# Attention whose value matmul turns around: values with ones columns as weights, one normalisation per head, no turns of the result

## The chip, the cores and the metric

The kernel runs on 1 core of one Trainium2 chip. The metric is the time of one execution on the device in microseconds (us), as a median over runs.

## What is computed

The program is a stack of transformer blocks for 512 tokens of width 1024. The change lies in the first mixer, an attention with 16 heads whose query and key have 96 numbers per head (64 without and 32 with rotary positions) and whose value has 64:

```python
q = (rms_norm(q_lat, q_norm) @ w_qb).reshape(B, S, H, QK_NOPE + QK_ROPE)
kv = (rms_norm(kv_lat, kv_norm) @ w_kvb).reshape(B, S, H, QK_NOPE + V_HEAD)
...
s = (jnp.einsum('bqhd,bkhd->bhqk', qn, k_nope)
     + jnp.einsum('bqhr,bkr->bhqk', qr, k_rope)).astype(jnp.float32) * scale
s = jnp.where(causal, s, MASK_VALUE)
p = jax.nn.softmax(s, axis=-1).astype(v.dtype)
...
o = jnp.einsum('bhqk,bkhd->bqhd', p, v)   # for each block of 128 queries
return o @ w_out
```

Everything is float32. The projections are done as three matmuls on two halves of each number (`hi` and `lo`), so each weight is split before its use: ScalarE makes `whi`, VectorE `wlo`.

## The kernel before, in words

The order on each engine is the order in which `mla_pe`, `mla_act` and `mla_dve` write it; semaphores alone tie the engines together. The heart is a loop of 68 steps over 64 units. A unit is one head `h` and one block `i` of 128 queries (`mla_units`); by causality it has `i + 1` blocks of keys, so its width is 128, 256, 384 or 512 columns. Eight steps, two heads, make a group; "position" below is the step number modulo 8, so positions 3 and 7 hold the widest units. In step `n`

- TensorE does the scores of unit `n`, turns the probabilities of unit `n-3` (`turn`, a transpose per key block), and multiplies those of unit `n-4` with the values (`values`). Between these come the matmuls of the next group's query and key projection (`mla_project`): ten triples of 512 columns, up to three of them in a step from position 1 on.
- VectorE adds the mask and takes the row maximum (one custom instruction, `prob<-ps,tab`), scales it (L347, the event `nm`), takes reciprocals of the row sums, and in between works at `modulation` (`part<-stage`, two instructions of 256 columns in a step, from step 2 to step 49), the lower halves of the weights (`dve_ahead`), and `queries` (four instructions of rotary work for two heads).
- ScalarE does the exponential with the row sum (`prob<-prob`), copies the turned probabilities to `probt`, the result times the reciprocal to `mlao` (`L.O`), splits weights and copies `mlaqh` and `mlakh`.

PSUM banks are handed out in turn by `take` and `banks`: five banks rotate over scores, turned probabilities and results, so whoever takes a bank waits until its use five takes ago is free. After the loop, 32 transposes turn `L.O`, ScalarE and VectorE split the outcome in `xhi` and `xlo`, then split the first pieces of `w_out`, and the output projection `wo` begins.

## Time and profile before

| | us |
|---|---|
| median of 3 runs | 3034.06 (3028.78 to 3034.18) |
| the profiled execution, its own time | 3029.49 |
| its span, first to last instruction | 3028.2 |
| TensorE busy | 2824.6 |
| VectorE busy | 1716.8 |
| ScalarE busy | 1235.5 |

Busy times are those of the whole program; the attention loop is the stretch from 110.2 to 297.0 us of the span. The profiled execution lies at the lower end of the runs.

### The profile page before, as it was taken

What the parts mean: (1) busy time and instruction counts of PE and PEld (TensorE: products, weight loads), DVE (VectorE), ACT (ScalarE), POOL (GpSimd) and SP (SyncE); (2) the same over time, 40 slices, a digit from 0 to 9 for tenths busy, and PEclk for the clock granted to TensorE, in tenths of its full rate; (3) what the DMA queues carried; (4) which work ended last, traced back from release to release, by engine and by line L of the source; (5) the groups of instructions that cost most, each with busy time, mean ns of one, the idle gap of its engine ahead of it and who ended that gap; (6) DMA issues with size and microseconds to landing.
All of it is one profiled execution on the core that took longest, in us unless ns stands there. A gap on an engine that the chain in (4) does not pass through costs nothing. (4 is left out here: it accounts for less than half of the span.)

```text
span 3028.2 us, 36283 instructions
## 1 busy us (share of the span) xinstructions
PE 2824.6 (93%) x14489; PEld 2311.1 (76%) x14489; DVE 1716.8 (57%) x2889; ACT 1235.5 (41%) x2128; POOL 247.4 (8%) x224
## 2 busy tenths in 40 slices
PE   7988999999997989899999997999999998899998
PEld 5766787787886978678877775788788766678886
DVE  6675554445864866543578886443425386744344
ACT  3556322223434344333467775432233345432222
POOL 0000000000003442010000010121100002100000
PEclk9899999999999999899999998999999999999999
DMA  5232344332231211154589994211330214422321
GB/s 227 89 110 87 111 182 153 132 113 89 106 138 42 71 43 43 50 204 146 188 317 360 345 369 156 81 49 60 101 113 32 84 35 134 144 72 87 112 80 66
DMA packets 72096, 387.66 MB, mean 128 GB/s; under 512 B 8234, under 2 KB 9934, under 8 KB 36174
## 3 DMA queue, kind: packets, MB, share of 16 engines
q1 hardware_dynamic: 58512, 349.20, 31.7%
q10 hardware_dynamic: 10382, 26.07, 2.5%
q0 software_dynamic: 3024, 9.98, 0.9%
q8 instruction: 116, 1.90, 0.3%
q14 instruction: 62, 0.51, 0.1%
HBM read 368.43 MB, written 22.03 MB: 129 GB/s over the span
## 5 line engine op out<-in xcount | busy, mean ns | idle before, releaser
L343 DVE TENSOR_TENSOR wlo<-stage,whi 128x1024 fp32r<-128x1024 f32 (+3 forms) x504 | 531.4, 1095 | 354.7 <-ACT whi L355 347.7
L355 ACT ACTIVATE whi<-stage 128x1024 fp32r<-128x1024 f32 (+3 forms) x504 | 440.5, 922 | 225.4 <-PE ps L639 195.5
L639 PE MATMUL ps<-bxhi,whi 128*128 128x512 f32 x480 | 200.9, 419 | 17.1 <-DVE bxlo L343 8.4
L639 PE MATMUL ps<-whi,mxhi 128*128 128x512 f32 (+1 forms) x528 | 204.3, 387 | 9.4 <-DVE wlo L343 7.3
L639 PE MATMUL ps<-whi,mxlo 128*128 128x512 f32 (+1 forms) x528 | 197.5, 374 | 0.0
L639 PE MATMUL ps<-wlo,mxhi 128*128 128x512 f32 (+1 forms) x528 | 197.4, 374 | 0.0
L639 PE MATMUL ps<-bxhi,wlo 128*128 128x512 f32 x480 | 190.1, 396 | 0.0
L639 PE MATMUL ps<-bxlo,whi 128*128 128x512 f32 x480 | 189.7, 395 | 0.0
L343 DVE TENSOR_TENSOR wlo<-more,whi 128x1024 fp32r<-128x1024 f32 (+1 forms) x126 | 142.2, 1171 | 44.3 <-ACT whi L355 43.7
L351 DVE SCALAR_TENSOR_TENSOR part<-stage,small,part 128x256 f32<-128x256 f32 x259 | 151.1, 583 | 9.2
L639 PE MATMUL ps<-lxhi,whi 128*128 128x512 f32 x352 | 141.2, 401 | 6.1 <-DVE lxlo L351 5.0
L639 PE MATMUL ps<-gwide 128*128 128x128 f32 x1088 | 134.3, 283 | 13.2 <-POOL gwide L343 10.2
L639 PE MATMUL ps<-fxhi,whi 128*128 128x512 f32 x352 | 139.7, 397 | 5.0 <-DVE fxlo L351 3.8
L639 PEld LDWEIGHTS ps<-gwide 128*128 128x128 f32 x1088 | 128.8, 197 | 16.2 <-POOL gwide L343 12.8
L639 PE MATMUL ps<-fxhi,wlo 128*128 128x512 f32 x352 | 138.6, 394 | 0.0
L639 PE MATMUL ps<-fxlo,whi 128*128 128x512 f32 x352 | 138.3, 393 | 0.0
L639 PE MATMUL ps<-lxhi,wlo 128*128 128x512 f32 x352 | 137.8, 391 | 0.0
L639 PE MATMUL ps<-lxlo,whi 128*128 128x512 f32 x352 | 137.7, 391 | 0.0
L355 ACT ACTIVATE whi<-more 128x1024 fp32r<-128x1024 f32 (+1 forms) x126 | 121.1, 1011 | 39.0 <-PE ps L639 36.0
L639 PEld LDWEIGHTS ps<-whi,mxhi 128*128 128x128 f32 x528 | 99.9, 189 | 38.5 <-DVE wlo L343 16.0
L639 PEld LDWEIGHTS ps<-bxhi,whi 128*128 128x128 f32 x480 | 91.9, 192 | 37.9 <-DVE bxlo L343 9.2
L639 PEld LDWEIGHTS ps<-whi,mxlo 128*128 128x128 f32 x528 | 99.9, 189 | 18.2
(597 smaller groups left out, 6283.9 us busy)
## 6 DMA issues: line engine op xcount, KB each, us to landing
stage<-in_gu SPq DMA_DIRECT2D x92, 1024.0 KB, 5.7
stage<-in_ada SPq DMA_DIRECT2D x40, 1024.0 KB, 5.0
more<-in_gu SPq DMA_DIRECT2D x40, 1024.0 KB, 6.7
stage<-in_dn SPq DMA_DIRECT2D x26, 768.0 KB, 4.5
stage<-in_dn SPq DMA_DIRECT2D x19, 1024.0 KB, 6.6
stage<-in_gin SPq DMA_DIRECT2D x16, 1024.0 KB, 4.9
stage<-in_gt SPq DMA_DIRECT2D x16, 1024.0 KB, 4.9
more<-in_dn SPq DMA_DIRECT2D x13, 1024.0 KB, 7.0
```

The source lines that it names most:

```text
L343: return e.do.tensor_tensor(out, x, y, op)
L351: return e.do.scalar_tensor_tensor(out, x, c, y, op0, op1)
L355: return e.do.activation(out, x, f, **kw)
L639: return self.p.do.matmul(out, lhsT, rhs, start=start, stop=stop, skip_group_check=True)
```

## The change

The value matmul swaps its operands. The values of a pair of heads now lie in SBUF as 64 columns of one head, 64 columns of ones, 64 columns of the other (`L.V`, the ones written once by GpSimd in `mla_pool`). A slice of 128 of these columns is the stationary operand, and the turned probabilities (128 columns) move. The result comes out turned, one PSUM bank per head for all four query blocks (`("oh", h)`, banks 3 and 4 by turns), with the row sums in the other 64 partitions. So the exponential no longer sums, the reciprocals and the copies to `mlao` go, and so do the 32 transposes after the loop. Once per head, behind its fourth block, ScalarE takes Ln and Exp(-x) of the row sums (`share`) and VectorE multiplies the head with them into `L.OT` (`weigh`). Scores and turned probabilities now rotate over three banks. On ScalarE the copy of unit `n-3` stands ahead of the exponential of unit `n`. The projections are spread over positions 1 to 6; the split of the key weights and the query work move to position 4, the key copies to position 6. The split of the result (`across_act`, `dve_low`) and the first two pieces of `w_out` move into steps 56 to 63.

```diff
@@ -834,8 +834,12 @@
         L = Space()
         L.X = tuple(self.at(n, [P, 8, 512], o, F32R) for n, o in (("xhi", 46), ("xlo", 54)))
         L.XK = tuple(t[:, 4:6, :] for t in L.X)
-        L.V, L.O = self.at("mlav", [P, 4, 1024], 62), self.at("mlao", [P, 4, 1024], 70)
-        L.raw = L.O[:, :, :].rearrange("p a b -> p (a b)").rearrange("p (m n) -> p m n", n=512)
+        L.V = self.at("mlav", [P, 4, 8, 192], 62)
+        ot = self.at("mlao", [P, 4, 512], 74)
+        early = [self.at(n, [P, 2, 512], o) for n, o in (("mlaoa", 52), ("mlaob", 60))]
+        L.OT = [early[i % 2][:, i // 2, :] for i in range(4)] + [ot[:, i, :] for i in range(4)]
+        low = self.at("mlaraw", [P, 4, 512], 84)
+        L.raw = [low[:, i, :] for i in range(4)] + [ot[:, i, :] for i in range(4)]
         L.cs = self.at("rope", [P, 2, 512], 78)
         L.q = [self.at("mlaq", [96, 4, 512], 80)[:, i, :] for i in range(1)]
         q, k = self.at("mlaqh", [96, 4, 512], 80), self.at("mlakh", [96, 4, 512], 84)
...
@@ -894,7 +899,7 @@
         self.pe_gemm_tok("wv", "wv", range(4), L.XE, self.normed("nk"))
         for _ in self.mla_project(L, 0):
             pass
-        self.banks(range(5))
+        self.banks(range(3))
         units = self.mla_units()
         more = None
 
@@ -915,35 +920,31 @@
 
         def values(n):
             h, i = units[n]
-            ps, vacant = self.take(("o", n))
-            p.wait_ge(*vacant, A(free(("t", n))), A(("v", h // 4, 3)))
+            if i == 0:
+                _, vacant = self.take(("oh", h), at=3 + h % 2)
+                p.wait_ge(*vacant)
+            ps, side = self.bank(("oh", h)), slice(64 * (h % 2), 64 * (h % 2) + 128)
+            p.wait_ge(A(free(("t", n))), A(("v", h // 4, 3)), self.G("ones"))
             for j in range(i + 1):
-                z = self.mm(ps[:, 0:64], L.pt[n % 4][:, j * P:(j + 1) * P], L.V[:, j, h * 64:h * 64 + 64], j == 0, j == i)
+                z = self.mm(ps[:, i * P:(i + 1) * P], L.V[:, j, h // 2, side], L.pt[n % 4][:, j * P:(j + 1) * P], j == 0, j == i)
             z.then_inc(*P_.up(("o", n)))
 
         for n in range(64 + 4):
-            if n % 8 == 0 and n < 56:
-                more = self.mla_project(L, n // 8 + 1)
-            step = more if n % 8 and n < 64 else iter(())
+            if n % 8 == 0:
+                more = self.mla_project(L, n // 8 + 1) if n < 56 else iter(())
             if n < 64:
                 scores(n)
-            next(step, None)
+            if n % 8 in (1, 2, 3, 4):
+                next(more, None)
             if 3 <= n < 67:
                 turn(n - 3)
-            next(step, None)
+            if n % 8 in (1, 2, 3, 4, 5, 6):
+                next(more, None)
             if n > 3:
                 values(n - 4)
-            next(step, None)
             if n >= 8 and (n - 8) % 4 == 0 and (n - 8) // 4 < 12:
                 self.pe_ada(0, 8 + (n - 8) // 4)
         self.banks(range(7))
-        for m in range(8):
-            ps, vacant = self.take(("ot", m))
-            p.wait_ge(*vacant)
-            for i in range(4):
-                p.wait_ge(A(free(("o", 4 * (2 * m + 1) + i))))
-                z = self.tr(ps[:, i * P:(i + 1) * P], L.O[:, i, m * P:(m + 1) * P])
-            z.then_inc(*P_.up(("ot", m)))
         for _ in self.pe_gemm("wo", "wo", range(4), L.X, lambda q: [V(("ot", "l", q))]):
             pass
...
@@ -1016,23 +1018,22 @@
                 k = (2 * g + h) % 4
                 act(a, L.k[k][0:64, :], self.bank(use)[64 * h:64 * h + 64, :], ACT.Copy).then_inc(*A.up(("ke", 2 * g + h), *([free(use)] if h else [])))
 
+        def share(h):
+            top, low = slice(64 * (h % 2), 64 * (h % 2) + 64), slice(64 - 64 * (h % 2), 128 - 64 * (h % 2))
+            r = L.tmp[2][top, :]
+            a.wait_ge(P_(("o", 4 * h + 3)), *([V(("od", h - 2))] if h > 1 else [V(("nq", "l", 3))]))
+            act(a, r, self.bank(("oh", h))[low, :], ACT.Ln).then_inc(*A.up())
+            a.wait_ge(A.now())
+            act(a, r, r, ACT.Exp, scale=-1.0).then_inc(*A.up(("share", h)))
+
         units = self.mla_units()
         self.act_ahead("wq", 0)
         queries(0)
         self.act_ahead("wk0", 0)
         keys(0)
+        self.act_ahead("wq", 1, False)
         for n in range(64 + 4):
             g = n // 8 + 1
-            if n < 64:
-                w = (units[n][1] + 1) * P
-                c, sl = L.cols[n % 6], L.sl[n % 5]
-                a.wait_ge(V(("nm", n)))
-                act(a, sl[:, 0:w], sl[:, 0:w], ACT.Exp, bias=c[:, 5:6], scale=L.scale, accum_out=c[:, 4:5]).then_inc(*A.up(("e", n)))
-            if n % 8 == 2 and g < 8:
-                self.act_ahead("wq", g, False)
-                self.act_ahead(f"wk{g}", 0, False)
-            if n % 8 == 4 and g < 8:
-                keys(g)
             if 3 <= n < 67:
                 u = n - 3
                 w = (units[u][1] + 1) * P
@@ -1040,26 +1041,43 @@
                 if u >= 4:
                     a.wait_ge(P_(("o", u - 4)))
                 act(a, L.pt[u % 4][:, 0:w], self.bank(("t", u))[:, 0:w], ACT.Copy).then_inc(*A.up(free(("t", u))))
-            if n % 8 == 3 and g < 8:
+            if n < 64:
+                w = (units[n][1] + 1) * P
+                sl = L.sl[n % 5]
+                a.wait_ge(V(("nm", n)))
+                act(a, sl[:, 0:w], sl[:, 0:w], ACT.Exp, bias=L.cols[n % 6][:, 5:6], scale=L.scale).then_inc(*A.up(("e", n)))
+            if n % 8 == 4 and g < 8:
+                self.act_ahead(f"wk{g}", 0, False)
                 queries(g)
+            if n % 8 == 6 and g < 8:
+                keys(g)
...
             if n > 3:
-                u = n - 4
-                h, i = units[u]
-                a.wait_ge(P_(("o", u)), V(("rl", u)))
-                if u < 4:
-                    a.wait_ge(V(("nk", "l", 1)))
-                act(a, L.O[:, i, h * 64:h * 64 + 64], self.bank(("o", u))[:, 0:64], ACT.Copy, scale=L.cols[u % 6][:, 6:7]).then_inc(*A.up(free(("o", u))))
+                h, i = units[n - 4]
+                if i == 3:
+                    share(h)
             if n % 8 == 7 and g < 7:
                 self.act_ahead("wq", g + 1, False)
-        for m in range(8):
-            if m == 0:
-                a.wait_ge(P_(("o", 63)))
-            self.act_high("ot", L.X, m, self.bank(("ot", m))[:, :], P_(("ot", m)))
+            if 56 <= n < 63:
+                self.across_act(L, n - 56)
+            if n in (61, 63):
+                self.act_ahead("wo", 0, n == 63)
+        self.across_act(L, 7)
         for n in range(4):
             self.act_ahead("wo", n)
             for m in (2 * n, 2 * n + 1):
                 self.act_square("wo", m, L.tmp[0:2], 1.0, *([V("posread")] if m == 0 else []))
         self.last_square = L.tmp[1], A(("wo", "q", 7))
+
+    def across_act(self, L, m):
+        marks = [self.V(("od", 2 * m)), self.V(("od", 2 * m + 1)), self.P((("k", 7), 0))]
+        if m > 5:
+            marks.append(self.V(("ot", "l", m - 6)))
+        self.act_high("ot", L.X, m, L.OT[m], *marks)
+
+    def mla_pool(self, L):
+        g = self.g
+        g.wait_ge(self.V(("mod", 0, 1)))
+        g.do.memset(L.V[:, :, :, 64:128], 1.0).then_inc(*self.G.up("ones"))
 
     def rope_angles(self, L, between):
         v, V, A = self.v, self.V, self.A
...
@@ -1157,6 +1175,7 @@
         self.dve_ahead("wq", 0)
         queries(0)
         self.dve_ahead("wk0", 0)
+        self.dve_ahead("wq", 1, False)
         v.wait_ge(self.Dt[0]("tab"))
 
         def modulation():
@@ -1164,6 +1183,12 @@
                 yield from self.dve_ada(0, n)
                 if n % 4 == 0 and n > 8:
                     self.dve_mod(0, n // 4 - 1)
+
+        def weigh(h):
+            top = slice(64 * (h % 2), 64 * (h % 2) + 64)
+            b = self.bank(("oh", h))
+            v.wait_ge(A(("share", h)))
+            tt(v, L.OT[h // 2][top, :], b[top, :], L.tmp[2][top, :], MUL).then_inc(*V.up(("od", h), free(("oh", h))))
 
         more = modulation()
         for n in range(64 + 4):
@@ -1174,31 +1199,30 @@
                 v.wait_ge(P_(("s", n)))
                 if n >= 5:
                     v.wait_ge(P_(("t", n - 5)))
-                if n >= 6:
-                    v.wait_ge(A(free(("o", n - 6))))
                 v.do.tensor_tensor_reduce(sl[:, 0:w], self.bank(("s", n))[:, 0:w], L.tab[:, 512 - w:512], 1.0, NEG, ADD, MAX, c[:, 0:1]).then_inc(
                     *V.up(free(("s", n))))
                 v.wait_ge(V.now())
                 ts(v, c[:, 5:6], c[:, 0:1], -L.scale, None, MUL).then_inc(*V.up(("nm", n)))
-            if n % 8 == 2 and g < 8:
-                self.dve_ahead("wq", g, False)
+            if n % 8 == 4 and g < 8:
                 self.dve_ahead(f"wk{g}", 0, False)
-            if n % 8 == 3 and g < 8:
                 queries(g)
             if n > 3:
-                c = L.cols[(n - 4) % 6]
-                v.wait_ge(A(("e", n - 4)))
-                v.do.reciprocal(c[:, 6:7], c[:, 4:5]).then_inc(*V.up(("rl", n - 4)))
+                h, i = units[n - 4]
+                if i == 3:
+                    weigh(h)
             if n % 8 == 7 and g < 7:
                 self.dve_ahead("wq", g + 1, False)
             if n > 1:
                 next(more, None)
+            if 56 <= n < 63:
+                self.dve_low("ot", L.X, n - 56, L.OT[n - 56])
+            if n in (61, 63):
+                self.dve_ahead("wo", 0, n == 63)
         for _ in more:
             pass
         self.dve_mod(0, 4)
         self.dve_gain("n2", 0, 3, "nf0")
-        for m in range(8):
-            self.dve_low("ot", L.X, m, self.bank(("ot", m))[:, :], P_(("ot", m)), done=[free(("ot", m))])
+        self.dve_low("ot", L.X, 7, L.OT[7])
         for n in range(4):
             self.dve_ahead("wo", n)
```

The first place is VectorE from the mask of position 3 on (`ISA prob` is the mask and maximum, `part<-stage` the modulation, `tmp<-ps,rope` and `mlaqh<-tmp` the query work). Before:

```order
L1179 ISA prob,small<-ps,tab 128x512 [waits s_matmuls]
L1179 ISA small 128x1
L347 TENSOR_SCALAR small<-small 128x1 [waits s_vector]
L343 TENSOR_TENSOR tmp<-ps,rope 64x512 [waits s_vector,s_matmuls]
L343 TENSOR_TENSOR tmp<-ps,rope 64x512
L343 TENSOR_TENSOR mlaqh<-tmp 32x512 [waits s_vector]
L343 TENSOR_TENSOR mlaqh<-tmp 32x512
L1191 RECIPROCAL small<-small 128x1
L351 SCALAR_TENSOR_TENSOR part<-stage,small,part 128x256 [waits s_vector] x2
```

In the changed kernel:

```order
L1202 ISA prob,small<-ps,tab 128x512 [waits s_matmuls]
L1202 ISA small 128x1
L347 TENSOR_SCALAR small<-small 128x1 [waits s_vector]
L343 TENSOR_TENSOR mlaob<-ps,tmp 64x512 [waits s_scalar]
L351 SCALAR_TENSOR_TENSOR part<-stage,small,part 128x256 [waits s_vector] x2
L1202 ISA prob,small<-ps,tab 128x128 [waits s_matmuls]
L1202 ISA small 128x1
L347 TENSOR_SCALAR small<-small 128x1 [waits s_vector]
L343 TENSOR_TENSOR wlo<-stage,whi 128x128 [waits s_scalar] x2
L343 TENSOR_TENSOR tmp<-ps,rope 64x512 [waits s_vector,s_matmuls]
L343 TENSOR_TENSOR tmp<-ps,rope 64x512
```

The multiplication with the share (`mlaob<-ps,tmp`), which waits for ScalarE, and the split of the key weights now stand ahead of the query work, and the mask of the next unit too.

The second place is ScalarE there, from the exponential of the widest unit on. Before:

```order
L355 ACTIVATE prob,small<-prob,small 128x512 [waits s_vector]
L355 ACTIVATE probt<-ps 128x128 [waits s_matmuls]
L355 ACTIVATE mlaqh<-ps 64x512 x2
L355 ACTIVATE mlao<-ps,small 128x64 [waits s_vector,s_matmuls]
L355 ACTIVATE prob,small<-prob,small 128x128 [waits s_vector]
L355 ACTIVATE mlakh<-ps 64x512 [waits s_matmuls]
L355 ACTIVATE mlakh<-ps 64x512
L355 ACTIVATE probt<-ps 128x256 [waits s_matmuls]
```

In the changed kernel:

```order
L355 ACTIVATE prob<-prob,small 128x512 [waits s_vector]
L355 ACTIVATE tmp<-ps 64x512 [waits s_matmuls]
L355 ACTIVATE tmp<-tmp 64x512 [waits s_scalar]
L355 ACTIVATE probt<-ps 128x256 [waits s_matmuls]
L355 ACTIVATE prob<-prob,small 128x128 [waits s_vector]
L355 ACTIVATE whi<-stage 128x128 [waits s_load2]
L355 ACTIVATE whi<-stage 128x128
L355 ACTIVATE mlaqh<-ps 64x512 x2
```

The Ln and the Exp of `share` (`tmp<-ps`, `tmp<-tmp`) follow the widest exponential; the key weights and the queries follow the next one.

The third place is TensorE at positions 4 and 5 (`small,prob` are the transposes, `mlav,probt` the values, `xhi,whi` a projection). Before:

```order
L642 MATMUL ps<-small,prob 128x128 x2
L639 MATMUL ps<-mlav,probt 128x64 [waits s_vector]
L639 MATMUL ps<-small,part 128x1 x2
L639 MATMUL ps<-mlakh,mlaqh 128x256
L642 MATMUL ps<-small,prob 128x128 [waits s_scalar]
L642 MATMUL ps<-small,prob 128x128 x2
L639 MATMUL ps<-mlav,probt 128x64 [waits s_scalar,s_vector]
L639 MATMUL ps<-mlav,probt 128x64
```

In the changed kernel:

```order
L642 MATMUL ps<-small,prob 128x128 [waits s_vector]
L642 MATMUL ps<-small,prob 128x128
L639 MATMUL ps<-xhi,whi 128x512
L639 MATMUL ps<-xlo,whi 128x512
L639 MATMUL ps<-xhi,wlo 128x512
L639 MATMUL ps<-probt,mlav 128x128 [waits s_scalar]
L639 MATMUL ps<-small,part 128x1 x2
L639 MATMUL ps<-mlakh,mlaqh 128x256
L642 MATMUL ps<-small,prob 128x128 [waits s_vector]
L642 MATMUL ps<-small,prob 128x128 x2
```

The transposes waited for ScalarE (`s_scalar`) and now wait for VectorE (`s_vector`), because of the rotation over three banks: `turn` takes the bank of the scores of the step before, which VectorE's mask frees.

## Rows read from the trace of the kernel before

**Rows 1.** The page: busy us, share of the span and instructions by engine.

```profile
PE 2824.6 (93%) x14489; PEld 2311.1 (76%) x14489; DVE 1716.8 (57%) x2889; ACT 1235.5 (41%) x2128; POOL 247.4 (8%) x224
```

**Rows 2.** Window: length, busy PE, PEld, DVE, ACT, POOL, clock, DMA, GB/s.

```profile
149.40:221.60 72.20, 60.83 (x344) 46.72 (x343) 52.36 (x170) 40.13 (x120) 0.00 (x0) 1.00 0.32 115
```

**Rows 3.** Two windows of 4 us early in the loop, same columns.

```profile
116.00:120.00 4.00, 2.29 (x10) 1.23 (x8) 3.25 (x9) 2.16 (x5) 0.00 (x0) 1.00 0.01 2
...
124.00:128.00 4.00, 3.32 (x12) 2.32 (x11) 1.83 (x8) 2.22 (x7) 0.00 (x0) 0.50 0.37 124
```

**Rows 4.** Timeline of PE: the score matmul that opens step 24, 32, 48, 56.

```profile
181.76 0.44 PE L639 MATMUL ps<-mlakh,mlaqh 96*128 96x128 f32 x2
...
205.81 0.44 PE L639 MATMUL ps<-mlakh,mlaqh 96*128 96x128 f32 x2
...
256.52 0.44 PE L639 MATMUL ps<-mlakh,mlaqh 96*128 96x128 f32 x2
...
279.52 0.44 PE L639 MATMUL ps<-mlakh,mlaqh 96*128 96x128 f32 x2
```

**Rows 5.** Timeline of PE, steps 21 to 28: values, the widest score, waits, one triple.

```profile
177.36 0.63 PE L639 MATMUL ps<-mlav,probt 128*128 128x64 f32 x4 [1.70 <-ACT probt L355]
...
179.58 1.08 PE L639 MATMUL ps<-mlakh,mlaqh 96*128 96x512 f32 x2
...
187.02 0.63 PE L639 MATMUL ps<-mlav,probt 128*128 128x64 f32 x4 [0.94 <-ACT probt L355]
...
194.43 1.00 PE L639 MATMUL ps<-mlav,probt 128*128 128x64 f32 x8
...
196.18 0.50 PE L639 MATMUL ps<-xhi,whi 128*128 128x512 f32 x1 [0.75 <-ACT mlaqh L355]
...
196.98 0.39 PE L639 MATMUL ps<-mlakh,mlaqh 96*128 96x128 f32 x2
```

**Rows 6.** Timeline of DVE, steps 23 to 28.

```profile
180.70 0.69 DVE L1179 CUSTOM_DVE_ANT_0 prob<-ps,tab 128x512 f32<-128x512 f32 x1 [0.30 <-ACT probt L355]
...
183.35 1.29 DVE L343 TENSOR_TENSOR wlo<-stage,whi 128x512 fp32r<-128x512 f32 x2 [1.70 <-ACT whi L355]
...
191.26 0.49 DVE L343 TENSOR_TENSOR wlo<-stage,whi 128x128 fp32r<-128x128 f32 x2 [1.42 <-ACT whi L355]
...
194.63 1.41 DVE L343 TENSOR_TENSOR tmp<-ps,rope 64x512 f32<-64x512 f32 x2 [0.61 <-PE ps L639]
...
196.07 1.40 DVE L343 TENSOR_TENSOR mlaqh<-tmp 32x512 f32<-32x512 f32 x2
...
197.70 1.01 DVE L351 SCALAR_TENSOR_TENSOR part<-stage,small,part 128x256 f32<-128x256 f32 x2
...
198.74 0.29 DVE L1179 CUSTOM_DVE_ANT_0 prob<-ps,tab 128x128 f32<-128x128 f32 x1
```

**Rows 7.** Timeline of ACT, the same steps.

```profile
181.62 0.72 ACT L355 ACTIVATE prob<-prob,small 128x512 f32<-128x512 f32 x1 [0.71 <-DVE small L347]
...
199.26 0.40 ACT L355 ACTIVATE prob<-prob,small 128x128 f32<-128x128 f32 x1 [1.19 <-DVE small L347]
```

**Rows 8.** Tile prob before the loop: a Ln out of PSUM, then an Exp (min/median/max ns).

```profile
L355 ACT ACTIVATE prob<-ps,small x2: 687/688/689, 34.5 to 66.4; 128x512 f32<-128x512 f32 x2
...
L355 ACT ACTIVATE prob<-prob x2: 630/630/631, 35.2 to 67.1; 128x512 f32<-128x512 f32 x2
```

**Rows 9.** Timeline of PE in a later stage: 128-column fp32 matmuls, eight back to back.

```profile
1073.38 1.06 PE L639 MATMUL ps<-qkv 128*128 128x128 f32 x8
```

**Rows 10.** Timeline of PE, ACT and DVE from the last values to the projection.

```profile
296.82 3.85 PE L642 MATMUL ps<-small,mlao 128*128 128x128 f32 x32
...
304.27 0.47 PE L639 MATMUL ps<-xhi,whi 128*128 128x512 f32 x1 [3.60 <-DVE wlo L343]
...
301.44 3.95 ACT L355 ACTIVATE whi<-stage 128x1024 fp32r<-128x1024 f32 x4
...
302.91 4.62 DVE L343 TENSOR_TENSOR wlo<-stage,whi 128x1024 fp32r<-128x1024 f32 x4
```

More of the change, by code:

```diff
@@ L856, in mla @@
                     (), [self.P(("sqx", 7))])
-        L.nq = Norm("nq", lambda m: L.raw[:, m, :], 4, L.rq, self.prm["qn"], None, L.X, L.tmp,
+        L.nq = Norm("nq", lambda m: L.raw[m], 4, L.rq, self.prm["qn"], None, L.X, L.tmp,
                     lambda m: [L.raw_ok(m)], [self.A("rsq")], (), [self.P(("win", 6))], [self.V("krope"), self.P("sumq")])
-        L.nk = Norm("nk", lambda m: L.raw[:, 4 + m, :], 2, L.rs, self.prm["kvn"], None, L.XE, [L.raw[:, 6, :], L.raw[:, 7, :]],
+        L.nk = Norm("nk", lambda m: L.raw[4 + m], 2, L.rs, self.prm["kvn"], None, L.XE, [L.raw[6], L.raw[7]],
                     lambda m: [L.raw_ok(4 + m)], [self.A("rsk")])
```

12 lines of the change are left out of this document (7 added, 5 removed).

## Prediction

> **What bounds the kernel now.** I read the page first: TensorE is busy for 93% of the span [rows 1], so most of the program is bound by TensorE, and what the change does counts only where TensorE waits. The reader should see that the attention loop is such a place: over 72.2 us (three groups) TensorE is busy for 60.8, VectorE for 52.4 and ScalarE for 40.1, at a granted clock of 1.00 [rows 2]. None is full, so three engines wait for each other in a ring. The timeline gives the length of a group: step 24 opens at 181.76 and step 32 at 205.81, so 24.05 us; the group without modulation work (steps 48 to 55) takes 279.52 - 256.52 = 23.0 [rows 4]. TensorE's waits in a group are 1.70, 0.94 and 0.75 [rows 5], and one of 0.32 beside them that isn't shown: 3.7 in all. The two largest, before values, end with ScalarE's copy to `probt`, which stood behind an exponential that waited for VectorE (1.19 at 199.26) [rows 7]. VectorE in turn waited 1.70 and 1.42 for `whi` [rows 6]. After the loop TensorE spends 3.85 on 32 transposes, idles 3.60 more, and starts the output projection at 304.27 [rows 10], 24.75 after step 56 opened [rows 4].
>
> **The value matmul costs the same.** Before, 160 fp32 matmuls of 64 moving columns, eight instructions (four matmuls) in 1.00; now 128 columns move. The nearest row for that shape is a later stage: eight instructions of 128 columns take 1.06 [rows 5, 9]. So 0.015 for each matmul, 160 x 0.015 = 2.4 at most over the whole loop, and 0 if only the tail of the last one differs. I take 0; the other bound is that of a rate in proportion to the columns, which the same two rows exclude. The Trainium skill, TensorE: Matmul & The Clock Gate, section on the back-to-back issue gap, gives an isolated gap that grows with the moving columns, N / 2.4 GHz + 2.5 ns: four passes of 64 more columns would by it be an estimated 0.107 us for each of 160 matmuls, 17 us in all. The same page puts a weight load of 128 columns at 128 / 1.2 = 107 ns, and by that the load, not the moving side, paces both forms; rows 5 and 9 agree with that.
>
> **What goes.** Eight reciprocals in a group (I price one at 0.1: under 1 us of VectorE), the read of the row sum and the copy to `mlao` on ScalarE. None lies where the new ring closes, so 0 on the path. The ScalarE copy ahead of the exponential removes the waits of 1.70 and 0.94 as they stand. The 32 transposes (3.85) and the 3.60 idle after them go from the end.
>
> **What comes.** Once per head Ln and Exp on ScalarE, 0.69 + 0.63 [rows 8], with hops of some 0.05 to each side 1.4; then the multiplication on VectorE out of PSUM, nearest row `tmp<-ps,rope`, 1.41 / 2 = 0.7 [rows 6]. VectorE's own work in a group thus grows by only 1.4 - 0.8, to about 18. But `weigh` of a head stands in the very step in which TensorE ends that head's last values, so VectorE stops for it, and behind it are queued the modulation, the next mask and, at position 4, the key weights and queries. Who waits for the masks is TensorE: with three banks `turn` of unit n-3 takes the bank of the scores of step n-1, so the transposes need the mask of the step before. Before, the five banks put that demand only on the values, a little later in the step. GpSimd writes the ones before the loop, when VectorE has nothing on the path: 0; if that cover were gone, one write of 2048 columns, a few us at most by POOL's other work.
>
> **One group of the changed kernel**, from the end of the values at position 7:
> - A. ScalarE is 0.4 late (the score at position 7 ends 1.2 before the values; mask to exponential 181.62 - 180.70 = 0.9 and exponential 0.7 follow it [rows 6, 7]); share 1.4; multiply 0.7; lower halves of the query weights 1.3; modulation 1.0; mask 0.3: TensorE's transposes at position 1 may start after 5.1.
> - B. TensorE from there to the end of the values at position 3. Before, 187.02 to 195.43 is 8.4 with six triples [rows 5]; now five (a triple 196.98 - 196.18 = 0.8 with its start, 0.7 in a row) and three transposes of 0.12 each (3.85 / 32 [rows 10]): 8.4 - 0.7 + 0.4 = 8.1.
> - C. Share 1.4; multiply 0.7; modulation 1.0; mask start to exponential 199.26 - 198.74 = 0.5; exponential 0.3; `whi` of the key weights 0.5 and VectorE's last half of them 0.3; queries 1.41 + 1.40 = 2.8; modulation 1.0; mask of 256 columns 0.5 [rows 6 to 8]. Sum 9.0, all in series, since each waits for the one before or stands behind it.
> - D. TensorE again: four transposes 0.5, the tenth triple 0.7, three value matmuls 0.7, the widest score 1.0 (1.08 with its tail [rows 5]), two transposes 0.2, four value matmuls 1.0: 4.1.
>
> Sum 26.3, against 24.05: +2.3. Steps 8 to 47 are five such groups, +11.5. In steps 48 to 55 the modulation ends after two steps, which takes 1.0 off A or C twice: 24.3 against 23.0, +1.3. The first group has one share only, at its end: 0. The loop up to step 56: +12.8.
>
> **The last steps.** From step 56 on no projection covers anything, and each step carries a split: exponential, `xhi` on ScalarE (0.5, as the Exp of 512 columns, 0.63, less its overlap with the next [rows 8]), then `xlo` on VectorE (0.65, as half of 1.29 [rows 6]), then the next mask, for which the transposes wait. Mask start to the next mask start is 0.5 + 0.3 + 0.5 + 0.7 = 2.0 for 128 columns, 2.3 and 2.6 for the next two, and 0.9 + 0.6 + 1.4 (share) + 1.3 = 4.2 for 512. The first mask waits for the share and multiplication of head 12: 2.5. Then 2.0 + 2.3 + 2.6 + 4.2 + 2.0 + 2.3 + 2.6 = 18.0, plus the first piece of `w_out` in step 61 (`whi` 3.95 / 4 = 1.0 and `wlo` 2.35 for two [rows 10], less the 0.7 it replaces: 2.6). Step 63: exponential 1.5 after its mask, share 1.4, two `whi` 2.0; then the copies and values of the last three units, 2.8. Together 30.8 from step 56 to the first matmul of the projection, against 24.75: +6.1. So the removed 7.3 at the end is paid with longer steps before it. The share of head 15 lies behind nine microseconds of matmuls that don't need it: 0.
>
> **Sum.** 12.8 + 6.1 = +18.9 on the profiled execution's 3029.49: 3048.4. That execution is 4.6 below the median of the runs; on the median it is 3053, which I forecast.
>
> **Rivals.**
> - *TensorE closes the loop (faster).* If VectorE reaches the masks in time, the transposes never wait and a group is TensorE's own work, 24.05 - 3.7 = 20.35, so -3.7 x 7 = -26; the last steps keep their 17.5 and lose 7.3: about 3001 by the median. For it: VectorE's work of 18 is under 20.35. It decides in C: the stretch from share to mask of position 5 must be under the TensorE work beside it, about 5 us (score, two triples, transposes, values); the rows give 9.0. Half of it (only position 3 stalls) lands near 3020. Chance 0.17.
> - *The ends cancel.* If VectorE makes up at positions 1 and 2 what it loses, a group stays near 24 and the last steps come out within 4 of before: 3028 to 3040. Chance 0.12.
> - *TensorE's clock falls more often.* The changed loop lets TensorE idle about 6 in 26 instead of 3.7 in 24, in gaps of 1.5 to 2. Before, TensorE was busy for only 2.29 of the 4.0 us from 116 on, and at 124 the clock stood at 0.50, that is at 1.2 GHz [rows 3]. B and D then run at half speed: about 12 us of a group. One fall of some 10 us in each of four more groups costs 4 x 4 = 16 more: 3062 to 3080. Chance 0.15. The Trainium skill (TensorE: Matmul & The Clock Gate, "What's actually happening") says that idleness brings the lower level and activity lifts it; the rows fit, since the fall came behind a pause.
> - *The forecast*, a ring over share, multiplication and masks: 3040 to 3064. Chance 0.53, and 0.03 for something slower still.
>
> A measurement of this kernel can tell about 0.2%, 6 us. Faster is the first rival with its half case, 0.17; same 0.12; slower 0.71. The range of 8 in 10 leaves out the faster rival's lower part and the clock's upper part: 3016 to 3074; the likeliest case alone is 3040 to 3064. The unknown costs (0 to 2.4 of the value matmul, 0.1 to 0.2 for each hop, some 12 in the ring: +-1 a group) lie inside.
>
> **What would show it.** After: step 24 to step 32 some 26 us; TensorE's longest waits before transposes (L642) ended by VectorE's mask; VectorE's longest wait ended by ScalarE's Exp in `tmp`, about 3 us at position 3; value matmuls 1.0 for eight; the first `xhi,whi` of the projection right behind the last values, 30 us after step 56 opens. Wrong if groups are 22 or less, if the transposes wait for nothing, or if eight value instructions take nearer 1.8.

## The result, and the profile after

The changed kernel takes 3062.7 us (median of 4 runs, 3059.74 to 3064.55) against 3034.12 for the kernel before (3028.78 to 3040.47). The ratio is 1.0096, 95% interval 1.0072 to 1.0121: some 29 us slower. The forecast was 3053, its likeliest case 3040 to 3064. The profiled execution of the changed kernel took 3063.30, its span 3062.0.

The page first, the rows that answer to [rows 1]; the columns are busy time, share of the span, instructions.

```profile
## 1 busy us (share of the span) xinstructions
PE 2839.1 (93%) x14457; PEld 2320.2 (76%) x14457; DVE 1722.4 (56%) x2841; ACT 1237.5 (40%) x2032; POOL 248.4 (8%) x225
```

They tell almost nothing: VectorE's and ScalarE's work is that of before within 6 us. The stretch of [rows 2] says more, and behind it stands one group, step 24 to step 32, cut into slices of 4 us. The columns are the length, each engine's busy time with its instructions, TensorE's granted clock, the DMA share and GB/s.

```profile
149.40:221.60 72.20, 56.61 (x289) 43.21 (x289) 48.62 (x134) 35.70 (x72) 0.00 (x0) 0.90 0.27 99
...
184.77:212.64 27.87, 21.55 (x117) 16.60 (x115) 18.07 (x51) 13.76 (x29) 0.00 (x0) 0.94 0.27 100
...
188.00:192.00 4.00, 2.86 (x9) 2.18 (x10) 3.75 (x13) 1.39 (x4) 0.00 (x0) 0.73 0.03 8
192.00:196.00 4.00, 4.00 (x21) 3.31 (x20) 2.28 (x7) 1.26 (x3) 0.00 (x0) 0.84 0.43 141
...
216.00:220.00 4.00, 2.99 (x10) 2.22 (x11) 3.75 (x13) 1.38 (x4) 0.00 (x0) 0.65 0.02 4
220.00:224.00 4.00, 4.00 (x13) 3.00 (x12) 2.15 (x7) 0.22 (x1) 0.00 (x0) 0.50 0.50 156
```

Every engine does less in the same 72.2 us than in [rows 2]: the loop waits more. And the clock, 1.00 in [rows 2], is now 0.90 over this stretch of some three groups, down to 0.50 in one slice. The next fence is TensorE's timeline through that group, the rows that answer to [rows 4, 5]; in brackets stand the idle time before an instruction and what ended it.

```profile
184.77 0.39 PE L639 MATMUL ps<-mlakh,mlaqh 96*128 96x128 f32 x2
...
188.26 0.50 PE L639 MATMUL ps<-xhi,whi 128*128 128x512 f32 x1 [1.78 <-DVE wlo L343]
...
190.11 0.90 PE L642 MATMUL ps<-small,prob 128*128 128x128 f32 x3 [0.89 <-DVE small L1202]
...
198.62 1.05 PE L639 MATMUL ps<-probt,mlav 128*128 128x128 f32 x8
199.51 0.39 PE L639 MATMUL ps<-mlakh,mlaqh 96*128 96x128 f32 x2
...
203.11 0.55 PE L642 MATMUL ps<-small,prob 128*128 128x128 f32 x3 [0.48 <-DVE small L1202]
205.23 0.50 PE L639 MATMUL ps<-xhi,whi 128*128 128x512 f32 x1 [1.57 <-DVE tmp L343]
...
208.91 0.66 PE L642 MATMUL ps<-small,prob 128*128 128x128 f32 x4 [1.61 <-DVE small L1202]
...
211.75 1.05 PE L639 MATMUL ps<-probt,mlav 128*128 128x128 f32 x8
212.64 0.39 PE L639 MATMUL ps<-mlakh,mlaqh 96*128 96x128 f32 x2
```

The group is 27.87 long (24.05 before). The waits before values are gone, as foreseen, and three waits now stand before the transposes (L642), each ended by VectorE's mask and maximum (L1202), with two more before triples, ended by VectorE too. Eight value instructions start 0.89 ahead of what follows them (211.75 to 212.64), though twice as many columns move; in the kernel before it was 0.91:

```profile
180.85 1.08 PE L639 MATMUL ps<-mlav,probt 128*128 128x64 f32 x8
181.76 0.44 PE L639 MATMUL ps<-mlakh,mlaqh 96*128 96x128 f32 x2
```

What VectorE did meanwhile in the changed kernel, from its timeline:

```profile
200.99 0.69 DVE L343 TENSOR_TENSOR mlaoa<-ps,tmp 64x512 f32<-64x512 f32 x1 [2.79 <-ACT tmp L355]
201.72 1.00 DVE L351 SCALAR_TENSOR_TENSOR part<-stage,small,part 128x256 f32<-128x256 f32 x2
202.76 0.29 DVE L1202 CUSTOM_DVE_ANT_0 prob<-ps,tab 128x128 f32<-128x128 f32 x1
...
203.91 0.49 DVE L343 TENSOR_TENSOR wlo<-stage,whi 128x128 fp32r<-128x128 f32 x2 [0.67 <-ACT whi L355]
204.51 1.41 DVE L343 TENSOR_TENSOR tmp<-ps,rope 64x512 f32<-64x512 f32 x2
205.95 1.40 DVE L343 TENSOR_TENSOR mlaqh<-tmp 32x512 f32<-32x512 f32 x2
207.38 1.00 DVE L351 SCALAR_TENSOR_TENSOR part<-stage,small,part 128x256 f32<-128x256 f32 x2
208.42 0.42 DVE L1202 CUSTOM_DVE_ANT_0 prob<-ps,tab 128x256 f32<-128x256 f32 x1
```

It stands still for 2.79, for ScalarE's Ln and Exp of the row sums, and from 200.99 it works up to the mask at 208.42 that TensorE wants, with one more pause, of 0.67, for ScalarE's `whi` of the key weights. That is the ring of the prediction's part C.

The end of the loop, TensorE and ScalarE:

```profile
295.76 0.39 PE L639 MATMUL ps<-mlakh,mlaqh 96*128 96x128 f32 x2
...
324.69 1.22 PE L639 MATMUL ps<-probt,mlav 128*128 128x128 f32 x4 [3.97 <-ACT probt L355]
325.70 1.06 PE L642 MATMUL ps<-small,prob 128*128 128x128 f32 x4
326.55 3.19 PE L639 MATMUL ps<-probt,mlav 128*128 128x128 f32 x14
329.40 0.67 PE L639 MATMUL ps<-xhi,whi 128*128 128x512 f32 x1
```

```profile
321.08 0.59 ACT L355 ACTIVATE tmp<-ps 64x512 f32<-64x512 f32 x1
321.70 0.63 ACT L355 ACTIVATE tmp<-tmp 64x512 f32<-64x512 f32 x1
322.24 1.98 ACT L355 ACTIVATE whi<-stage 128x1024 fp32r<-128x1024 f32 x2
324.25 0.77 ACT L355 ACTIVATE probt<-ps 128x256 f32<-128x256 f32 x2
```

The projection starts 33.64 after step 56 opens (24.75 before). Set against the profiled execution of before, the 25.1 by which it starts later come together like this: the first group (110.2 to 127.73) is 17.53 in place of 22.74, -5.2; steps 8 to 47 take 142.14 (127.73 to 269.87) in place of 123.60, +18.5; steps 48 to 55 take 25.89 in place of 23.0, +2.9; and the end +8.9.

### The profile page after: what moved, and what is told of

Same layout as the page of the kernel before. It is cut to its first block and busy times, and to the rows that moved or that the text cites. A ratio compares the mean times of both kernels' runs of the same rounds, so it can differ in the third digit from the quotient of the medians.

```text
span 3062.0 us, 35915 instructions
## 1 busy us (share of the span) xinstructions
PE 2839.1 (93%) x14457; PEld 2320.2 (76%) x14457; DVE 1722.4 (56%) x2841; ACT 1237.5 (40%) x2032; POOL 248.4 (8%) x225
## 5 line engine op out<-in xcount | busy, mean ns | idle before, releaser
L639 PE MATMUL ps<-xhi,whi 128*128 128x512 f32 x200 | 94.5, 472 | 25.9 <-DVE wlo L343 10.7
```

Of the source, the lines that this page charges most:

```text
L639: return self.p.do.matmul(out, lhsT, rhs, start=start, stop=stop, skip_group_check=True)
```

## The experiments

"Group" is a mean over the five of steps 8 to 47, "end" the time from the opening of step 56 to the first matmul of the output projection, both from the profiled execution. A clean group before is 24.05; the mean is 24.7, since three of the five ran partly at a lower clock. Each ratio is to runs of the kernel before on the same chip, whose median was 3032.0 to 3034.1; the kernels ran on several chips, so compare ratios rather than medians.

| kernel | median, us | ratio, 95% interval | group | end |
|---|---|---|---|---|
| before | 3034.1 | | 24.7 | 24.75 |
| changed | 3062.7 | 1.0096 (1.0072 to 1.0121) | 28.4 | 33.6 |
| e1_weigh_later | 3047.7 | 1.0045 (1.0029 to 1.0060) | 25.4 | 32.1 |
| e2_banks | 3051.3 | 1.0054 (1.0035 to 1.0073) | 26.7 | 34.2 |
| e3_fill | 3046.8 | 1.0044 (1.0031 to 1.0057) | 26.4 | 33.7 |
| e4_wo_late | 3062.6 | 1.0088 (1.0064 to 1.0112) | 28.3 | 31.1 |
| e5_before_wide | 3029.4 | 0.9991 (0.9978 to 1.0004) | 24.6 | 24.8 |
| e6_across_late | 3057.7 | 1.0089 (1.0068 to 1.0109) | 28.4 | 27.6 |
| e7_open_ring | 3037.6 | 1.0019 (1.0004 to 1.0034) | 24.9 | 32.7 |
| e8_ring_late | 3026.7 | 0.9982 (0.9969 to 0.9995) | 24.8 | 24.2 |
| e8_again | 3029.9 | 0.9989 (0.9976 to 1.0002) | 24.2 | 24.8 |
| e9_ring_fill | 3023.0 | 0.9960 (0.9945 to 0.9974) | 23.5 | 25.0 |
| e10_fill_wo_late | 3021.8 | 0.9963 (0.9947 to 0.9978) | 23.5 | 24.9 |
| e11_before_fill | 3029.3 | 0.9987 (0.9973 to 1.0001) | 24.1 | 25.9 |

**Does the ring close through the multiplication?** e1_weigh_later moves VectorE's multiplication with the share (`weigh`) from the step of the head's last values to the step after, behind that step's mask and ahead of the key weights and queries.

```diff
+            if n % 4 == 0 and n > 7:
+                weigh(n // 4 - 2)
             if n % 8 == 4 and g < 8:
...
-            if n > 3:
-                h, i = units[n - 4]
-                if i == 3:
-                    weigh(h)
...
+        weigh(15)
```

> The changed kernel, with VectorE's multiplication of a head (weigh) moved one step later, behind the mask of positions 4 and 0; ScalarE and TensorE keep their order. Ring theory: at position 3 VectorE no longer stops 2.8 us for ScalarE's Exp; the mask and exponential of position 4 come earlier, bounded by ScalarE's own order (share 1.4, then the copy 0.3, then the exponential), so part C of the prediction goes from 9.2 to about 7.2. At position 7 nothing is won, since VectorE then stops for whi, which ScalarE makes behind the share. A group goes from 27.9 to 25.5 to 26.5, the kernel is 12 to 15 us faster than the changed one. Rival, that the wait only moves to another instruction and the three banks or the clock set the pace: group and time stay within 3 us of the changed kernel.

The group fell from 28.4 to 25.4 and the median by 15 us. VectorE's waits ahead of the multiplication fell from 2.79 and 2.07 a group to 0.57 and 0. The place of that one instruction was half of the loss.

**Does the demand for the mask come from the three banks?** e2_banks gives the scores two banks by turns and the turned probabilities the third, so that a transpose no longer needs the bank of the scores just before it.

```diff
-            ps, vacant = self.take(("s", n))
+            ps, vacant = self.take(("s", n), at=n % 2)
...
-            ps, vacant = self.take(("t", n))
+            ps, vacant = self.take(("t", n), at=2)
```

> The changed kernel, with the scores on two PSUM banks by turns and the turned probabilities on the third, in place of one rotation over three. Then the transposes of step n don't need the mask of step n-1; the scores of step n need the mask of step n-2. If the bank rotation closes the ring: TensorE's waits before the transposes (L642) go, two value groups and a transpose slip into the stall at positions 1 and 6, a group goes from 27.9 to about 24.5, the kernel is some 20 us faster than the changed one. Rival, that VectorE's chain (share, multiply, key weights, queries) sets the pace whatever the banks: the waits move from the transposes to the scores, a group stays above 27.

It did what it should to the transposes and gained 11 us, but the groups came to 26.7 and not to the 24.5 that was expected. TensorE's timeline of this kernel, with every wait of step 24 to 32:

```profile
180.33 0.46 PE L639 MATMUL ps<-mlakh,mlaqh 96*128 96x128 f32 x2 [0.68 <-ACT mlakh L355]
181.16 0.44 PE L642 MATMUL ps<-small,prob 128*128 128x128 f32 x2 [0.37 <-ACT probt L355]
184.36 0.50 PE L639 MATMUL ps<-xhi,whi 128*128 128x512 f32 x1 [1.66 <-DVE wlo L343]
200.37 0.50 PE L639 MATMUL ps<-xhi,whi 128*128 128x512 f32 x1 [2.27 <-DVE tmp L343]
```

In this group no wait before a transpose is longer than 0.37. The long ones moved to the projection's triples, which need what stands behind the multiplication in VectorE's queue (the query weights' lower half, the rotary work that frees a bank). The late engine is the same; only the instruction that meets it is another.

**What does the clock cost?** e3_fill adds matmuls that nobody reads where TensorE waits, and changes nothing else.

```diff
+        def fill(k):
+            for _ in range(k):
+                w = 256 if n % 4 == 1 else 128
+                self.mm(self.bank(("oh", (n - 4) // 4))[:, 512 - w:512], self.c("ones"), self.x[:, 0, 0:w])
...
+            if 8 <= n < 64:
+                fill({1: 2, 6: 3}.get(n % 8, 0))
             if n % 8 in (1, 2, 3, 4):
                 next(more, None)
+            if 8 <= n < 64:
+                fill({1: 1}.get(n % 8, 0))
             if 3 <= n < 67:
                 turn(n - 3)
+            if 8 <= n < 64:
+                fill({5: 2}.get(n % 8, 0))
```

> The changed kernel with matmuls nobody needs in TensorE's waits from step 8 on: two fp32 matmuls of 256 columns ahead of the first projection triple of position 1 and one behind it, two of 256 at position 5 behind the transposes, three of 128 at position 6 ahead of the transposes, about 3.3 us in a group, into columns that the values of later blocks overwrite. Theory that the clock's falls in the loop (granted 0.5 to 0.8 in one or two 4-us windows of each group) come from these waits and make the difference of the forecast's 26.3 and the measured 27.9 a group: the clock stays at 1.00, a group falls to about 26.3, 8 to 10 us less for the kernel. Rival, that the falls have nothing to do with how TensorE waits there: the clock still falls, and a group is 27.9 or, since a filler stands ahead of work at half speed, up to 28.5.

The granted clock is 1.00 all through steps 8 to 55, the groups are 26.4, 26.39, 26.4, 26.38, 26.4, and the median is 16 us below the changed kernel's. From step 56 on it fell again (0.65 from 296 to 300, 0.50 from 312 to 316), and the end stayed at 33.7. The whole group from 179.67 on, and TensorE's rows at its turning points:

```profile
179.67:206.07 26.40, 22.88 (x133) 17.90 (x131) 18.00 (x51) 13.76 (x29) 0.00 (x0) 1.00 0.30 105
```

```profile
178.78 1.05 PE L639 MATMUL ps<-probt,mlav 128*128 128x128 f32 x8
179.67 0.39 PE L639 MATMUL ps<-mlakh,mlaqh 96*128 96x128 f32 x2
...
185.01 0.55 PE L642 MATMUL ps<-small,prob 128*128 128x128 f32 x3 [0.46 <-DVE small L1213]
...
192.05 1.05 PE L639 MATMUL ps<-probt,mlav 128*128 128x128 f32 x8
192.94 0.39 PE L639 MATMUL ps<-mlakh,mlaqh 96*128 96x128 f32 x2
...
202.35 0.66 PE L642 MATMUL ps<-small,prob 128*128 128x128 f32 x4 [0.95 <-DVE small L1213]
...
206.07 0.39 PE L639 MATMUL ps<-mlakh,mlaqh 96*128 96x128 f32 x2
```

This is the group as the prediction built it, with the clock's part taken away. Measured: A 185.01 - 179.67 = 5.3 (5.1 forecast), B 192.94 - 185.01 = 7.9 (8.1), C 202.35 - 192.94 = 9.4 (9.0), D 206.07 - 202.35 = 3.7 (4.1); 26.4 against 26.3. The parts are each up to 0.4 off, and their errors cancel in the sum.

**The end of the loop.** e4_wo_late splits the first pieces of `w_out` in step 67 rather than in 61 and 63; e6_across_late splits the result (`xhi`, `xlo`) behind the loop.

```diff
-            if n in (61, 63):
-                self.dve_ahead("wo", 0, n == 63)
+            if n == 67:
+                self.dve_ahead("wo", 0)
```

```diff
-            if 56 <= n < 63:
-                self.dve_low("ot", L.X, n - 56, L.OT[n - 56])
...
-        self.dve_low("ot", L.X, 7, L.OT[7])
+        for m in range(8):
+            self.dve_low("ot", L.X, m, L.OT[m], *([self.V(("ot", "l", m - 3))] if m > 5 else []))
```

(and the same on ScalarE in both, in e6_across_late with one wait between the two engines moved along).

> The changed kernel with the split of the first two pieces of w_out moved from steps 61 and 63 to step 67 on both engines. Theory that these splits stand ahead of copies and masks that the last units need: step 56 to the first matmul of the projection takes 33.6 in the changed kernel; without the 2.6 at step 61 and the 2.0 at step 63 but with a first split of 1.0 + 1.2 behind the last copy, about 30.5, so 3 us less. Rival, that the splits were hidden: 33.6 plus 1 to 2, slower by that.

> The changed kernel with the split of the result in xhi and xlo (across_act, dve_low) moved from steps 56 to 62 behind the loop, as before the change; the pieces of w_out stay in steps 61 and 63. Theory that these splits stand in the ring of the last steps (each step waits for exponential, xhi, xlo, next mask): step 56 to the first matmul of the projection goes from 33.6 to 26 to 28, since 7 x 1.2 leave the steps and only 1.3 comes behind the last values; the kernel is about 6 us faster than the changed one. Rival, that the share at every fourth step and the pieces of w_out set the last steps: within 2 us of the changed kernel.

The end is 2.5 shorter in e4_wo_late and 6.1 in e6_across_late. So of the 8.9 that it had grown by, the split of the result inside the last steps is two thirds. The medians don't show it clearly: 3062.6 and 3057.7 with ratios whose intervals overlap the changed kernel's.

**Do twice the moving columns cost anything?** e5_before_wide is the kernel before with 128 columns of values moving in place of 64, of which it still uses 64.

```diff
-                z = self.mm(ps[:, 0:64], L.pt[n % 4][:, j * P:(j + 1) * P], L.V[:, j, h * 64:h * 64 + 64], j == 0, j == i)
+                z = self.mm(ps[:, 0:P], L.pt[n % 4][:, j * P:(j + 1) * P], L.V[:, j, h // 2 * P:h // 2 * P + P], j == 0, j == i)
```

> The kernel before, with 128 moving columns in each value matmul (the values of both heads of a pair) in place of 64; ScalarE reads the head's 64 columns of the result. Theory that the weight load paces both forms: eight value instructions in a row take 0.9 to 1.0 as before, a group 24.05, no difference that can be measured. Rival, a rate in proportion to the moving columns: 0.1 for each of 160 matmuls, eight instructions 1.8, a group 2 longer, the kernel up to 16 us slower.

The ratio is 0.9991, and the upper end of its interval leaves at most 1.2 us of cost. Two groups took 24.05 and 24.07, as before. The other three took 24.39, 24.30 and 26.29; the last two had a wait of another kind, since ScalarE stood for 1.73 and 2.15 for the key weights to land (0.3 to 0.4 in the other groups and in the kernel before), and in the longest the clock fell too. So 128 moving columns cost no more than 64. That ends at 128: in e9_ring_fill, below, four instructions with 256 moving columns start 0.87 ahead of what follows them, 0.22 each for the 0.11 of 128 columns.

```profile
199.90 1.03 PE L639 MATMUL ps<-x,small 128*128 128x256 f32 x4
200.77 0.38 PE L642 MATMUL ps<-small,prob 128*128 128x128 f32 x2
```

**Both doors at once.** e7_open_ring has e2_banks' banks and puts `share` and `weigh` at the end of the step after the head's last values, on VectorE behind the modulation; the split of the query weights at position 7 thus comes ahead of them. e8_ring_late adds e6_across_late's split behind the loop; e8_again is that kernel once more.

```diff
-            if n > 3:
-                h, i = units[n - 4]
-                if i == 3:
-                    share(h)
+            if n % 4 == 0 and n > 7:
+                share(n // 4 - 2)
...
-            if n > 3:
-                h, i = units[n - 4]
-                if i == 3:
-                    weigh(h)
+            if n > 1:
+                next(more, None)
+            if n % 4 == 0 and n > 7:
+                weigh(n // 4 - 2)
             if n % 8 == 7 and g < 7:
                 self.dve_ahead("wq", g + 1, False)
-            if n > 1:
-                next(more, None)
```

> The changed kernel with both links of the ring opened: ScalarE's share of a head at the end of the next step (behind exponential, key weights and queries), VectorE's multiplication at the end of that step behind the modulation, at position 7 the split of the query weights ahead of them; and the PSUM banks of e2 (scores on two, turned probabilities on one). Theory that the 26 to 28 us of a group come from this ring and no engine's own work: VectorE waits no longer for the Exp, a group falls under 24, to 22 to 23.5, 25 to 35 us less than the changed kernel and thus as fast as the kernel before or faster. Rival, that VectorE with its 18 us of work and its waits for whi is the bound in any order: 25 or more, as e1.

> e7 with the split of the result behind the loop as in e6. If the two places are independent, the gains add: a group as in e7, step 56 to the projection 24 to 27, and the kernel is faster than the one before by 5 to 15 us (ratio 0.995 to 0.998). Rival: without the splits the last steps only wait longer for the share and the pieces of w_out, and e8 equals e7.

> A repeat of e8_ring_late without a change, beside the other two on one chip: ratio 0.998 again, between 0.9965 and 0.9995. A ratio of 1.000 or above would say that its gain over the kernel before doesn't stand.

VectorE now multiplies without waiting at position 4 and after a wait of 0.71 at position 0 (2.79 and 2.07 in the changed kernel). The groups of e7_open_ring, 24.9, missed the expected 22 to 23.5: its clock still fell in each of the five, to 0.50 to 0.79 over a slice of 4 us. With the ring opened alone (e7_open_ring) the end is still 32.7; with the split behind the loop it is 24.2. VectorE's timeline of e8_ring_late at position 4 and after, and two slices of its clock:

```profile
195.77 1.41 DVE L343 TENSOR_TENSOR tmp<-ps,rope 64x512 f32<-64x512 f32 x2
...
199.68 0.69 DVE L343 TENSOR_TENSOR mlaoa<-ps,tmp 64x512 f32<-64x512 f32 x1
200.41 0.42 DVE L1201 CUSTOM_DVE_ANT_0 prob<-ps,tab 128x256 f32<-128x256 f32 x1
```

```profile
204.00:208.00 4.00, 2.77 (x15) 2.06 (x16) 2.75 (x9) 2.79 (x6) 0.00 (x0) 0.98 0.84 346
208.00:212.00 4.00, 4.00 (x15) 3.20 (x14) 3.09 (x9) 2.62 (x5) 0.00 (x0) 0.59 0.02 4
```

The two sets of runs give 0.9982 and 0.9989, and the second's interval includes 1: that this kernel is faster than the one before, by some 3 to 6 us, is likely and not shown beyond doubt; 5 to 15 had been expected. In its two profiled executions the groups in which the clock fell took 24.3 to 26.0. In the second (e8_again) the clock stood at 1.00 from 188 to 280 us; there the last two of the five groups took 22.99 and 23.26, and steps 48 to 55 took 20.96.

**And the clock again.** e9_ring_fill is e8_ring_late with unread matmuls in the waits left, e10_fill_wo_late that with `w_out`'s pieces two and four steps later, e11_before_fill the kernel before with unread matmuls in its longer waits.

```diff
+        def fill(n):
+            k, w = {7: (2, 128), 0: (2, 256), 1: (3, 256)}.get(n % 8, (0, 0))
+            b = self.ps[6] if n % 8 == 0 else self.bank(("oh", (n - 4) // 4))
+            for _ in range(k):
+                self.mm(b[:, 512 - w:512], self.c("ones"), self.x[:, 0, 0:w])
```

```diff
-            if n in (61, 63):
-                self.dve_ahead("wo", 0, n == 63)
+            if n in (63, 67):
+                self.dve_ahead("wo", 0, n == 67)
```

```diff
             next(step, None)
+            if n < 62:
+                fill({3: 1, 5: 3}.get(n % 8, 0) if n != 3 else 3)
             if n > 3:
                 values(n - 4)
```

> The kernel of e8_ring_late with matmuls that nobody reads in TensorE's waits: two of 128 moving columns at position 7, two of 256 at position 0 and three of 256 at position 1 of steps 8 to 63, into a spare bank. That the granted clock still costs something in the loop (its windows stood at 0.50 to 0.69 at 208 to 212, 232 to 236 and 256 to 264 us): it stands at 1.00 from step 8 on, a group takes 23.0 to 23.8 us in place of 24.4 to 26, and the median comes out 5 to 8 us under e8_ring_late's, near 3020 us, ratio 0.996. Rival, that in this kernel the chain runs through VectorE and ScalarE where TensorE is slow: the clock is 1.00 but groups stay at 24.4, median 3026. Rival, that the added matmuls stand ahead of one that the chain needs: groups of 25 and more, slower than e8_ring_late.

> The kernel of e9_ring_fill with the two halves of the output weights' split at steps 63 and 67 in place of 61 and 63. If the split holds up the last steps' turned copies (in the changed kernel 1.98 us of it stood ahead of the copy that the last values wait for), the projection starts 1 to 2 us nearer to the opening of step 56: 22 to 23 us. Rival, that the first projection matmul then waits for the split itself: 24 to 26 us, and a median 0 to 2 us above e9_ring_fill's.

> The kernel before, with matmuls of 256 moving columns that nobody reads in TensorE's longer waits: three in step 3, one in position 3 and three in position 5 of the later groups. It says how much of the gain of e9_ring_fill (0.996) is the clock's alone. If the ring of the changed kernel's share and masks is what idled TensorE, the kernel before has little to gain: its clock fell in two stretches only (120 to 140 and 228 to 238 us), so the groups come to 24.05 throughout and the first to 20.65 or less, 2 to 6 us in all, median 3026 to 3030, ratio 0.998 to 0.9995. Rival, that the clock costs the kernel before as much as the changed one: ratio 0.996 or less.

e9_ring_fill, step 24 to 32 (the busy time of TensorE counts the added matmuls):

```profile
175.94:199.61 23.67, 22.45 (x129) 17.99 (x129) 18.06 (x51) 13.47 (x29) 0.00 (x0) 1.00 0.36 119
```

The groups are 23.43 to 23.72 at a clock of 1.00, the first kernel of all these with every group under the clean 24.05, and the median is 3023.0, 9 us under the kernel before and 7 under e8_again on the same chip. The added matmuls are not free, though: where e8_again had a full clock without them, its groups were 22.99 and 23.26, and steps 48 to 55 took 20.96, against 21.92 here. Moving the weights' split (e10_fill_wo_late) changes neither the end (24.9 for 25.0) nor the median by what can be told: its theory fell. The kernel before with a full clock has groups of 24.06, 24.08, 24.06, 24.08 and 24.06, and its ratio of 0.9987 can't be told from 1. So 0.996 isn't the clock's alone: at the same clock the turned value matmul, in an order in which VectorE doesn't stop for the share, has groups 0.5 us shorter (23.5 for 24.07), and the stretch from the first scores to the projection is 181.5 for 188.9. The two kernels were timed beside the kernel before, not beside each other, and the intervals of their ratios just touch (0.9945 to 0.9974 and 0.9973 to 1.0001).

## Why the prediction was right, and where it was not

- **The sign and the mechanism: right.** The new place of the waits (transposes, ended by VectorE's mask), VectorE's pause at position 3 (2.79, forecast about 3) and the value matmul's cost of 0 stand in the rows. e1_weigh_later, which takes only the pause away, and e2_banks, which takes only the demand away, each give back a part. The first rival (TensorE closes the loop, groups of 20.35) was never near: with the share and multiplication out of the way and the clock full, e9_ring_fill still has 23.5.
- **The value matmul: 0, shown.** By the isolated gap of the Trainium skill (TensorE: Matmul & The Clock Gate, "Back-to-back issue gap") the sum would have had an estimated 17 us; e5_before_wide leaves at most 1.2. Eight such instructions start 0.91 ahead of the next with 64 columns and 0.89 with 128. That agrees with the prediction's reading that the weight load paces them; no run here varied the load, and e5_before_wide widens the moving side without swapping the operands.
- **A to D: right in size**, 26.3 against 26.4 at full clock, the last tenths by luck: A came out 0.2 over and C 0.4 over, B 0.2 and D 0.4 under. Five groups at 2.35 over 24.05 are 11.7 (11.5 forecast), and steps 48 to 55 took 24.32 in e3_fill (24.3 forecast).
- **The clock: the rival that came on top.** The prediction kept "the clock falls more often" as a case of its own, 0.15, with 4 x 4 = 16 more. It was no case beside the forecast but a part of it: the ring's waits brought the clock down in every group, and filling them gives back 16 us on the medians (3062.7 to 3046.8), of which the stretch up to the projection shows 11.7 in the profiled pair (219.2 to 207.5 from the first scores on). The condition stood there (idle 6 in 26, in gaps of 1.5 to 2); the chance was too small. The measured 3062.7 lies both in this rival's range (3062 to 3080) and in the forecast's (3040 to 3064), so the time alone can't tell them apart; e3_fill does. The trace shows what came ahead of the falls: TensorE has eleven waits of 1.78 or 1.57 before triples in steps 8 to 55, ended by `wlo` or by the rotary work; right behind eight of them, all six of 1.78 among these, the clock fell. It did not fall behind three of the five of 1.57, nor right behind the waits of 1.61 to 1.63 before transposes (181.05, 208.91, 266.15), so no length of wait by itself decides it here. In e3_fill no wait is over 0.96 in steps 8 to 55, and there it never fell. So in the group shown B took 9.4 in the changed kernel (190.11 to 199.51) in place of 7.9, while A, C and D, where the clock was full or TensorE waited, stayed at 5.3, 9.4 and 3.7.
- **The base of the groups.** I counted five groups of 24.05 before. Their sum is 123.60 and not 120.3, since its own clock fell twice, at 120 to 138 and at 228 to 238 (of the first fall [rows 3] have a piece). So +18.5 in steps 8 to 47 is 21.9 over clean groups: 11.7 of the ring (e3_fill's five groups sum to 131.97) and 10.2 of the clock.
- **The first group: not foreseen.** Forecast 0, measured -5.2. e11_before_fill brings the kernel before from 22.74 to 19.23 there and e3_fill leaves the changed one at 17.5, so more than half was the fall of before's clock at 120 to 138, which the changed kernel doesn't have; the rest goes with the new order (projections spread, weights split ahead of the loop), and no run took that apart.
- **The last steps: mechanism right, 2.8 too short.** From the first mask (298.52) to the last (319.42) it took 20.9, forecast 18.0 + 2.6 = 20.6. The opening took 2.8 for 2.5, and from the last mask to the projection 10.0 for 7.7: exponential, share and `whi` (1.98 for two, as forecast) came on time, but the copies and values of the last three units took 5.15 (324.25 to 329.40) for 2.8. TensorE had stood idle for 3.97 and ran at a clock of 0.50 from 324 to 328. Its 22 instructions from 324.69 took 4.7; at the 0.11 each of a full clock that is an estimated 2.4, so the clock is enough to explain what was missing. No run kept it up there, so this is not shown by an experiment.
- **The rest of the program.** The median difference is 28.6, the stretch up to the projection explains 25.1 of one pair. What lies outside the stretch from the first scores to the projection took 2834.1 in the profiled execution before (3028.2 - 304.27 + 110.18), 2842.8 in that after, 2839.5 in e5_before_wide, 2836.1 in e8_again and 2851.1 in e11_before_fill, whose later code is before's word for word. It wanders by more than the 3.5 left, and nothing says that the change touches it.
- **Luck in the total.** Over the profiled pair 25.1 was measured for 18.9. The terms that were missing or too small are the clock's part (+11.7: 10.17 in steps 8 to 47 and 1.57 in steps 48 to 55, against e3_fill) and the end (+2.8). Against them stand two that were not foreseen either, the shorter first group (-5.2) and the falls of the clock in the kernel before (-3.4). Without these two the forecast would have been some 15 us too low on this pair, and not 6.

## What to carry to other kernels

Where three engines hand a tile round, price the ring from wait to wait, as in A to D, and not by busy time: the sum came out within 0.1 us of a group, its parts within 0.4, although no engine was full. Then ask what the new pauses do to TensorE's clock and add that to the same case, since it isn't an alternative to the ring but its consequence. And an instruction that waits for another engine belongs behind those that a third one needs: one VectorE multiplication moved by one step was worth 15 us, while moving the demand alone (the banks) was worth 11 and shifted the rest of the wait to the next instructions in that queue.

## What was not expected of the hardware

- Unread matmuls in waits kept the granted clock at 1.00 in every slice of steps 8 to 55 of four kernels (e3_fill, e9_ring_fill, e10_fill_wo_late, e11_before_fill) and cost little: five groups of the kernel before with them are 24.06 to 24.08, the clean group without them is 24.05. They are not free everywhere: at a clock of 1.00 both ways, steps 48 to 55 took 23.43 with them and 23.00 without in the kernel before, and 21.92 (e9_ring_fill) and 20.96 (e8_again) in the other order.
- The clock fell behind short pauses, but not each time: in e8_ring_late the waits between 203.3 and 207.2 are 0.68, 0.37 and 0.85, and the slice from 208 on stood at 0.59. In e8_again, the same kernel, the waits from 200.6 to 204.5 are again 0.68, 0.37 and 0.85, and the clock stayed at 1.00.
- fp32 matmuls with 64 and with 128 moving columns take the same time: eight instructions 0.91 and 0.89 from their start to the next one's, and e5_before_wide is not slower. With 256 columns each instruction takes twice as long (0.22 for 0.11).
